# A decoder step on one core: every second key page of the sample attention is loaded in 32-row blocks, and VectorE transposes the blocks

## The reference, cut to what matters

```python
z = (jnp.einsum('bqhd,bkhd->bhqk', q_blk.astype(jnp.float32), k.astype(jnp.float32)) * (SB_HEAD_DIM ** -0.5)
     + bias.astype(jnp.float32)[None, :, None, None])
```

## Time and profile before

| what | value |
|---|---|
| median of 3 runs | 2364.03 us (2361.04 to 2366.49) |
| the profiled execution, its own time | 2363.2 us |
| its span in the trace | 2361.5 us |
| mean granted clock of PE | 0.988 |
| PE busy | 2272.0 us (96%) |
| DVE busy | 1644.3 us (70%) |
| ACT busy | 1057.1 us (45%) |
| POOL busy | 48.9 us (2%) |
| DMA queue of SP | 326.16 MB, 44.5% of 16 engines over the span |

### The profile page before, as it was taken

The page is one execution under the profiler, slowest core; times in us unless marked ns, Lnnn a source line. Parts: engine busy times, 40 slices in busy tenths (PEclk is TensorE's granted clock), DMA queues, the critical chain, the costliest instruction groups (busy, mean ns, idle before and its releaser), DMA issues. The chain is left out here.

```text
span 2361.5 us, 47384 instructions
## 1 busy us (share of the span) xinstructions
PE 2272.0 (96%) x18644; PEld 2019.1 (86%) x18644; DVE 1644.3 (70%) x2774; ACT 1057.1 (45%) x1919; POOL 48.9 (2%) x108
## 2 busy tenths in 40 slices
PE   7999999999999999999969999899999999999998
PEld 7999999987879888888858866578999999997786
DVE  7766766656885487677657898657676766655886
ACT  7322222234554667566645555435522323233453
POOL 0000000000000100000010001010000000000000
PEclk9999999999999999999979999899999999999999
DMA  5343333365463233233258878723243432437454
GB/s 161 103 137 117 108 128 102 116 214 187 134 187 108 63 75 69 54 59 74 37 153 294 277 254 310 235 79 118 59 159 102 130 121 87 151 116 237 128 166 153
DMA packets 356274, 328.40 MB, mean 139 GB/s; under 512 B 103929, under 2 KB 264057, under 8 KB 356112
## 3 DMA queue, kind: packets, MB, share of 16 engines
q1 hardware_dynamic: 356112, 326.16, 44.5%
HBM read 254.63 MB, written 71.47 MB: 138 GB/s over the span
## 5 line engine op out<-in xcount | busy, mean ns | idle before, releaser
L1242 PE MATMUL a_q<-a_uh,a_p_hi 128*128 128x352 f32 x672 | 233.6, 348 | 0.6 <-ACT a_xp L1333 0.6
L1244 PE MATMUL a_q<-a_uh,a_p_lo 128*128 128x352 f32 x672 | 216.6, 322 | 0.0
L1243 PE MATMUL a_q<-a_ul,a_p_hi 128*128 128x352 f32 x672 | 216.1, 322 | 0.0
L1242 PEld LDWEIGHTS a_q<-a_uh,a_p_hi 128*128 128x128 f32 x672 | 126.6, 188 | 23.5 <-issue 21.6
L1243 PEld LDWEIGHTS a_q<-a_ul,a_p_hi 128*128 128x128 f32 x672 | 127.1, 189 | 0.1
L1244 PEld LDWEIGHTS a_q<-a_uh,a_p_lo 128*128 128x128 f32 x672 | 126.2, 188 | 0.0
L884 PE MATMUL c_q<-c_b_hi,c_a_hi 128*128 128x512 f32 x264 | 105.4, 399 | 3.9 <-DVE c_a_lo L783 3.0
L884 PE MATMUL a_q<-a_b_hi,a_a_hi 128*128 128x512 f32 x264 | 103.7, 393 | 3.2 <-DVE a_a_lo L783 3.0
L885 PE MATMUL c_q<-c_b_hi,c_a_lo 128*128 128x512 f32 x264 | 104.7, 396 | 0.0
L886 PE MATMUL c_q<-c_b_lo,c_a_hi 128*128 128x512 f32 x264 | 104.6, 396 | 0.0
L886 PE MATMUL a_q<-a_b_lo,a_a_hi 128*128 128x512 f32 x264 | 102.9, 390 | 0.0
(11 more groups left out here) (735 smaller groups left out, 7635.9 us busy)
## 6 DMA issues: line engine op xcount, KB each, us to landing
b_page<-in_cache_k SPq DMA_DIRECT2D x128, 256.0 KB, 4.2
b_page<-in_cache_v SPq DMA_DIRECT2D x128, 256.0 KB, 4.3
a_w_raw<-in_ffn_gu SPq DMA_DIRECT2D x44, 512.0 KB, 5.1
c_w_raw<-in_ffn_gu SPq DMA_DIRECT2D x44, 512.0 KB, 5.0
a_a_raw<-hid_rows SPq DMA_DIRECT2D x66, 256.0 KB, 2.7
c_a_raw<-hid_rows SPq DMA_DIRECT2D x66, 256.0 KB, 2.7
a_p_raw<-in_w_in SPq DMA_DIRECT2D x28, 512.0 KB, 4.2
a_raw_d<-in_ffn_d SPq DMA_DIRECT2D x11, 1024.0 KB, 5.0
```

The source lines that it names most:

```text
L1242: nc.tensor.matmul(self.pm[at % 2][:, 0:TB], wh, self.uh[t][:, c], start=(c == 0), stop=False)
L1243: nc.tensor.matmul(self.pm[at % 2][:, 0:TB], wh, self.ul[t][:, c], start=False, stop=False)
L1244: mm = nc.tensor.matmul(self.pm[at % 2][:, 0:TB], wl, self.uh[t][:, c], start=False, stop=(c == KC - 1))
```

## The change: what it does

- Key pages of b = 1, 3 are loaded in a block layout, with one transfer each as before. Partition 32i + t//4 receives, for dimension chunk i (of 128) and the four keys t = 4(t//4) + s, the 128 numbers of chunk i of each key. The source is walked as 4 chunks x 128 keys x 128 numbers, the destination is the whole 128 x 512 slot. Pages of b = 0, 2 and all value pages are loaded as before.
- VectorE transposes each of these pages with one instruction, 32x32 block by block, from `page` straight into `k_turned`, in place of the copy from PSUM. It waits for the page itself. PE transposes b = 0, 2 alone, still over three banks.
- In `scores` the moving operand of b = 1, 3 is a strided view of `k_turned`: 32 columns apart by one number, repeated for s with a step of 128 numbers. The contraction chunk c then holds dimensions 128i + 32c + r on partition 32i + r, so the queries and the new keys of b = 1, 3 are needed in the same order: `qs_b` and `ks_b`, loaded with four transfers each. DVE writes `qb` with 32 copies in place of 16.
- A slot of keys is free when PE's transposes and VectorE's are both counted. PE's waits for `q_ready` and `masks_out` move from the head of its list to the first scores.

```diff
-        qs, ks = s.sb("qs", [P, 4, T_S]), s.sb("ks", [P, 4, T_S])
+        qs, ks, qs_b, ks_b = (s.sb(n, [P, 4, T_S]) for n in ("qs", "ks", "qs_b", "ks_b"))
...
             sp.dma_start(qs[:], q_cols.rearrange("c p n -> p c n")).then_inc(E("q_cols_in"), 16)
+            for i in range(4):
+                sp.dma_start(qs_b[rows_in(i)], q_cols[i].rearrange("(c r) n -> r c n", r=R)).then_inc(E("q_cols_in"), 16)
             sp.dma_start(ks[:], k_cols.rearrange("c p n -> p c n")).then_inc(E("small_in"), 16)
+            for i in range(4):
+                sp.dma_start(ks_b[rows_in(i)], k_cols[i].rearrange("(c r) n -> r c n", r=R)).then_inc(E("small_in"), 16)
...
-                        sp.wait_ge(E("k_turned1"), 2 * old + 2)
+                        sp.wait_ge(E("k_turned0"), 2 * old + 2)
+                        sp.wait_ge(E("k_copied1"), 2 * old + 2)
...
-                        sp.dma_start(page[:, n % SLOTS, b:b + 1, :], src.rearrange("g p n -> p g n")).then_inc(E(f"page_in{n % SLOTS}"), 16)
+                        if keys and b % 2 == 1:
+                            sp.dma_start(page[:, n % SLOTS, b], src.rearrange("g t (i d) -> i (g t) d", d=P)).then_inc(E(f"page_in{n % SLOTS}"), 16)
+                        else:
+                            sp.dma_start(page[:, n % SLOTS, b:b + 1, :], src.rearrange("g p n -> p g n")).then_inc(E(f"page_in{n % SLOTS}"), 16)
...
-                        for e in range(2):
-                            b = 2 * half + e
-                            q = 4 * n + b - 3
-                            at_least(pe, E(f"k_copied{q % 2}"), q // 2 + 1)
-                            for c in range(4):
-                                mm = nc.tensor.transpose(pk[(4 * n + b) % 3][:, c], page[:, n % SLOTS, b, c * P:(c + 1) * P], ident[:])
-                            mm.then_inc(E(f"k_turned{e}"), 1)
+                        at = 2 * n + half
+                        at_least(pe, E("k_copied0"), at - 2)
+                        for c in range(4):
+                            mm = nc.tensor.transpose(pk[at % 3][:, c], page[:, n % SLOTS, 2 * half, c * P:(c + 1) * P], ident[:])
+                        mm.then_inc(E("k_turned0"), 1)
+
+            def keys_of(n, b, c):
+                if b % 2 == 0:
+                    return k_turned[n % 2][:, b, c]
+                return k_turned[n % 2][:, b, :, rows_in(c)].rearrange("p s t -> p t s")
...
+                    if p == 0:
+                        pe.wait_ge(E("q_ready"), gi + 1)
+                    if r == 0:
+                        pe.wait_ge(E("masks_out"), 1)
...
-                        dve.wait_ge(E("k_turned1"), 2 * n + half + 1)
-                        nc.vector.tensor_copy(k_turned[n % 2][:, 2 * half + 1], pk[(4 * n + 2 * half + 1) % 3][:]).then_inc(E("k_copied1"), 1)
+                        if half == 0:
+                            dve.wait_ge(E(f"page_in{n % SLOTS}"), page_count(n))
+                        nc.vector.transpose(k_turned[n % 2][:, 2 * half + 1].rearrange("p c n -> p (c n)"),
+                                            page[:, n % SLOTS, 2 * half + 1]).then_inc(E("k_copied1"), 1)
...
-            dve.wait_ge(E("q_cols_in"), 16)
+            dve.wait_ge(E("q_cols_in"), 80)
```

More of the change, by code:

```diff
@@ L2455, in rows_in, with page_count @@
             return slice(w * j, w * j + w)
+        def page_count(n):
+            return 64 * (n // SLOTS + 1)
         def flat_in(t):
@@ L2723, in turn_keys @@
                         if half == 0:
-                            pe.wait_ge(E(f"page_in{n % SLOTS}"), 64 * (n // SLOTS) + 64)
-                        for e in range(2):
-                            b = 2 * half + e
-                            q = 4 * n + b - 3
-                            at_least(pe, E(f"k_copied{q % 2}"), q // 2 + 1)
-                            for c in range(4):
-                                mm = nc.tensor.transpose(pk[(4 * n + b) % 3][:, c], page[:, n % SLOTS, b, c * P:(c + 1) * P], ident[:])
-                            mm.then_inc(E(f"k_turned{e}"), 1)
+                            pe.wait_ge(E(f"page_in{n % SLOTS}"), page_count(n))
+                        at = 2 * n + half
[7 more added lines that the diff above has]
+                return k_turned[n % 2][:, b, :, rows_in(c)].rearrange("p s t -> p t s")
             def products(out, gi, moving):
@@ L2746, in scores @@
                             pe.wait_ge(E(f"k_copied{e}"), 2 * (PAGES * gi + p) + 2)
-                        products(flat(pz[r % 2])[:, 0:P], gi, lambda b, c: k_turned[(PAGES * gi + p) % 2][:, b, c])
+                        products(flat(pz[r % 2])[:, 0:P], gi, lambda b, c: keys_of(PAGES * gi + p, b, c))
                     else:
-                        products(flat(pz[r % 2])[:, 0:T_S], gi, lambda b, c: ks[:, c])
+                        products(flat(pz[r % 2])[:, 0:T_S], gi, lambda b, c: (ks, ks_b)[b % 2][:, c])
             def values():
@@ L2772, in values @@
                 yield value_time(G, 0) + PE_AT["values"][2]
-                pe.wait_ge(E("k_copied1"), 2 * len(KEY_ROUNDS))
+                pe.wait_ge(E("k_copied0"), 2 * len(KEY_ROUNDS))
                 for gi in range(G):
@@ L2779, in _ @@
             pe.wait_ge(E("masks_made"), 1)
-            pe.wait_ge(E("small_in"), 48)
+            pe.wait_ge(E("small_in"), 112)
             nc.tensor.matmul(first[:, 0:1], pick_t[:], bias[:], start=True, stop=True)
@@ L2786, in _ @@
             mm.then_inc(E("masks_turned"), 1)
-            pe.wait_ge(E("q_ready"), G)
-            pe.wait_ge(E("masks_out"), 1)
             interleave(invert(), advance(), gates(), prepare(), scores(), turn_keys(), values())
@@ L2896, in key_copies @@
                         act.wait_ge(E("k_turned0"), 2 * n + half + 1)
-                        nc.scalar.activation(k_turned[n % 2][:, 2 * half], pk[(4 * n + 2 * half) % 3][:], ACT.Copy).then_inc(E("k_copied0"), 1)
+                        nc.scalar.activation(k_turned[n % 2][:, 2 * half], pk[(2 * n + half) % 3][:], ACT.Copy).then_inc(E("k_copied0"), 1)
             def weigh():
@@ L3189, in _ @@
             dve.wait_ge(E("qb_zero"), 1)
-            dve.wait_ge(E("q_cols_in"), 16)
+            dve.wait_ge(E("q_cols_in"), 80)
             for gi in range(G):
                 for h in range(H_SB):
-                    c, e = h // 2, h % 2
-                    src = qs[e * DH:(e + 1) * DH, c, 16 * gi:16 * gi + 16].rearrange("p (b q) -> p b q", q=L_S)
-                    step = nc.vector.tensor_copy(qb[e * DH:(e + 1) * DH, gi, c, :, L_S * h:L_S * h + L_S], src)
+                    c, e, to = h // 2, h % 2, slice(L_S * h, L_S * h + L_S)
+                    src = qs[e * DH:(e + 1) * DH, c, 16 * gi:16 * gi + 16].rearrange("p (b o q) -> p b o q", o=2, q=L_S)
+                    nc.vector.tensor_copy(qb[e * DH:(e + 1) * DH, gi, c, :, to].rearrange("p (b o) q -> p b o q", o=2)[:, :, 0], src[:, :, 0])
+                    k, pair = rows_in(c), slice(2 * e, 2 * e + 2)
+                    src = qs_b[k, pair, 16 * gi:16 * gi + 16].rearrange("p c (b o q) -> p c b o q", o=2, q=L_S)
+                    step = nc.vector.tensor_copy(qb[k, gi, pair, :, to].rearrange("p c (b o) q -> p c b o q", o=2)[:, :, :, 1], src[:, :, :, 1])
                 step.then_inc(E("q_ready"), 1)
```

## The result

The changed kernel takes 2512.53 us (median of 4 runs, 2510.99 to 2515.22), the kernel before 2363.89 (4 runs): a ratio of 1.0626, with a 95% interval from 1.061 to 1.0643. It is slower by 148.6 us. The profiled execution took 2514.05 us, its span is 2511.2 us, its mean granted clock 0.958.

A forecast was written before the change was run, and what follows sets the result against it. PE bounds the key rounds now, DVE and transfers close behind; four DMA engines would take over with 294.2 us. With start and tail the rounds end 143 us later: 2363.2 + 143 = 2506 us, range 2465 to 2550.

The forecast's parts named there:

- the likeliest case: Key rounds: block pages on four DMA engines make these the bound, 2506 us; chance 0.92, of which 0.80 near the forecast.
- Four engines, always the same: Block page transfers: outermost count 4 gives 4 engines, the same for all, 3.62 us a page.
- The sum of 294.2 us: Four engines' load in key rounds: 64 block pages 231.4 us, 64 plain pages 44.9, other transfers 17.9.
- The start: Before the key pages: eight more small loads take 3.6 us, so the first page is issued at 1221.8, not 1218.2.
- The tail: After the last key page lands: transposes, copy, products, logits and the round of new keys, 4.1 us.
- Behind the key rounds: Value rounds and later: what follows is unchanged, value rounds again 121 us; a lower clock could cost a few us.
- DVE's transposes: Key rounds on DVE: 64 block transposes of 128x512 at 0.71 us replace copies of 684 ns, +2 us.
- The strided operand: Products of b = 1, 3 on PE: between nothing and a doubling of 34.6 us, inside PE's slack, taken as nothing.
- 16 engines: Rival on block page transfers: 16 engines carry them, the kernel gains 5 to 20 us, 2351; chance 0.05 with a gain.
- The second rival: Key rounds, 16 engines: strided operand adds 34.6 us to PE's 110, nothing gained, about 2366; chance 0.03.
- What would show it: Key rounds: DMA share about 0.4, some 140 GB/s, rounds some 9 us apart, block pages well over 10 us to landing.
- three more rounds, some 27 us: SP's queue in key rounds: when SP reloads a slot, three more rounds' transfers, some 27 us, are still queued.

The follow-up runs named there:

- the version with a count of 2: Changed kernel, but each block page comes in two transfers of 64 partitions, each with an outermost count of 2: 2726.53 us.
- the engines' work: Changed kernel with all pages loaded in the plain layout, VectorE's transposes and the strided operand kept: 2364.27 us, ratio 0.9997 to the kernel before.
- the mended kernel with 512 B pieces: Changed kernel with plain-order pages, 512 B pieces for b = 1, 3, contiguous operand, sums written 4 numbers apart in PSUM: 2359.03 us, ratio 0.9979 to the kernel before.

## Why the prediction was right

The forecast was 2506.0 us (2465 to 2550), the time is 2512.5, and the likeliest case came true by its own mechanism. Its steps:

- **Four engines, always the same.** Right. It rested on one store of 27 rows. The changed kernel shows two to three tenths of the engines busy at 82 GB/s, and the version with a count of 2 shows one tenth at 41. The Trainium skill's rule ("DMA: Bandwidth & Descriptors", section "Why a DMA increments its semaphore by 16 and not by 1") says the same, and the trace agrees at both counts as to how many engines there are.
- **The sum of 294.2 us.** Right in total, and by some luck. From the first page issue (1222.8) plus 1.9 us to the last landing (1516.8) are 292.1 us. Its two main terms are each off by some 0.4 us, in opposite directions. While a block page moves alone it runs at 82 GB/s, which is 3.2 us and not 3.62. But a pair of pages takes 4.26 us, as the packets of a stretch without other loads show, 1300 to 1335 us:

```profile
DMA packets 5501, 4.48 MB, mean 128 GB/s; under 512 B 174, under 2 KB 4382, under 8 KB 5498
```

  4382 - 174 = 4208 pieces of 512 B are 8.2 block pages in 35 us. So the plain page and the hand-over to and from it take 1.06 us on the four engines, and not 0.70. The Trainium skill's other statement on that page (section "Specifications"), line rate from 512 B on, would have given 2.80 us a page and a time 52 us lower. The block page alone lies between the two, and the pair of pages sides with the sum (4.32).
- **The start.** The first page issue came at 1222.8, not 1221.8: the eight added loads take SP 3.9 us (0.48 each), in place of 3.6, and SP's list for this stage begins 0.8 us later than before (1212.3 against 1211.6).
- **The tail.** 9.8 us from the last landing to the last logits' start, in place of 4.1. Behind the last transposes (1.1 us) PE's list holds the products of the round before, at 1517.8, and pieces of the DeltaNet; the last round's own products start at 1522.7 and take 2.0 us (with the strided operand) in place of 1.1, and more of the DeltaNet stands ahead of the new keys. The forecast counted the last round's work alone. The clock has no part in it: from 1516 to 1526 the mean granted clock is 1.00.
- **Behind the key rounds.** Start (1.0) and tail (5.7), less the 2.1 us by which the sum was too high, are 4.6 of the 8 us by which the profiled execution passes the forecast. Most of the rest lies in the value rounds. "What follows is unchanged" held for the first half of them; the last product of the value rounds starts at 1653.0, 151.4 us later than before, not 147.8. From 1580 to 1600 us the mean granted clock is 0.83, where the like stretch before, 1432 to 1452, has 1.00, and 2.9 us of the 3.6 are lost there. The span's end makes up 1.7 us of it (it comes 149.7 us later), and 1.2 us more lie outside the span. The prediction named a cost of the clock in the value rounds and took nothing for it.
- **DVE's transposes.** 0.69 us taken together, against 0.71, and the lower bound, 0.684, was the better guess.
- **The strided operand.** I took nothing, with a doubling of 34.6 us as the bound. It is nearly the doubling, 31.2 us, and it was hidden as argued: with it taken away the changed kernel stays at 2513.65.
- **The rivals.** 16 engines would not have given 2351. As written, the engines' work gives 2364.3; with the operand mended and 512 B pieces, 2359.0. The second rival (the strided operand eats the gain, 2366) was the right one of the two, and I gave it the smaller chance. I had also put the key rounds at 126 to 140 us with DVE and the transfers competing, and they take some 141: in the mended kernel with 512 B pieces the logits run from 1237.9 to 1372.6 us, 8.9 us less than before. The 4 to 7 us lost at the start are 2.4 in the run with the engines' work alone (first logits at 1237.6 against 1235.2).
- **What would show it.** The GB/s (140 forecast, 141 measured) and the 256 records are right. So are the rounds some 9 us apart: PE's turns of the first and of the last round start at 1235.9 and 1516.8, 31 rounds at 9.1 us. The value rounds are 3.6 us longer than before, as said above. The DMA share is 0.51, not 0.41: packets of one engine overlap a little, so that the share is 0.28 while a block page moves alone (1301.1 to 1303.7 us), and not 0.25, and a piece of 2 KB takes a mean of 110 ns (1300 to 1335 us), where it took 86 before (1246 to 1250 us). Block pages don't take well over 10 us to landing: the last is issued at 1508.7 and has landed by 1516.8, 8 us, and in 30 of the 32 rounds PE turns the pages at most 8.7 us after the issue of the last one. That sign came from the queue that the next point corrects.
- **Missed altogether: SP's queue.** The plain page's issue behind a block page has a median of 2.77 us (L2506), where 0.33 is usual. SP doesn't run ahead of four busy engines by "three more rounds, some 27 us"; it is held up at its own instruction, and some 8 us, two block pages, are queued. This costs nothing here: in the slices of 1300 to 1304 us above the transfers never pause.

## What to carry to other kernels

Before a transfer's layout is changed, look at the outermost count of both its patterns: where the largest number up to 16 that divides it is small, few engines carry the transfer (4 for a count of 4, 2 for 2, and 9 for the 27 rows), on SP's queue always the same ones, and everything behind them waits (4 engines cost 149 us here, 2 engines 361). Splitting such a transfer moves the cost to the issuing queue, so count its issues and their pieces too. And when an engine's work is made cheaper by another layout, price the reads of that layout: here the strided operand gave back 31.2 of 32.4 us, where the stride in the output would have been almost free.

## What the runs showed of the hardware

- **An issue's time grows with its pieces.** On SP's queue a transfer with 128 pieces of 512 B takes 563 ns and one with 64 takes 317. A plain page, 128 rows of 2 KB, takes 333, and a block page, 512 pieces in one transfer, 597. So the number of pieces is not all of it. Behind a transfer on few engines, the next issue lasts a median of 2.77 us.
- **A moving operand with a step of 512 B between numbers** doubles the busy time of the f32 products of 128 columns (17.3 to 33 us for 512 records, only half of which walk the step), while a step of 16 B in the PSUM output, again for half of them, adds 1.2 us to 34.6. The Trainium skill ("SBUF — State Buffer", section "Door 1: The DMA port swizzle (why `[64,N]` ≈ `[32,N]`)") describes the first as a penalty on each access that leaves a 16-byte line, and the trace agrees. The Trainium skill also says there that any non-contiguous PSUM pattern slows matmuls significantly; for these f32 products the trace disagrees, and the measurement decides.
- **A 32x32-block transpose of 128x512 f32** takes VectorE 0.69 us, as long as a copy of that size, while 128x128 takes 0.31.
- **A block page issued by GpSimd** takes it 1.57 us, and lands a median of 20.1 us later. The load then spreads over the engines, at a share above 1 with little to show for it (169 GB/s).
